# Mixer attention of a two-layer encoder: leaving out the TensorE products whose results are never read

## The reference, cut to what matters

```
u = rms_norm(x, g[MIX_PRE])
pa, pb, pc = jnp.split(u @ w_in[l], [split_b, split_c], axis=-1)
ya = neighbourhood_attn(qa * scale, ka, va, na_rpb[l])      # A: 6 heads
yb = hyena_mixer(pb, ...)                                   # B: 256 channels
yc = dilated_mixer(qc * scale, kc, vc, t5_table)            # C: 6 heads
y = jnp.concatenate([rms_norm(ya, ..), rms_norm(yb, ..), rms_norm(yc, ..)], axis=-1)
x = x + rms_norm(y @ w_out[l], g[MIX_POST])
```

## Time and profile before

| | |
|---|---|
| median of 3 runs | 2685.17 us (2684.04 to 2689.0) |
| the profiled execution: its own time | 2689.14 us |
| its span | 2687.3 us |
| mean granted TensorE clock of it | 0.98 of full speed |
| mixer attention, steps 2 to 54, layer 1 | about 632 to 739 us |
| mixer attention, steps 2 to 54, layer 2 | about 1960 to 2067 us |

### The profile page before, as it was taken

How to read it: one execution, slowest core, us unless ns; L and a number is a source line. 1 busy time by engine, 2 the same in 40 slices (tenths; PEclk the granted TensorE clock), 3 DMA queues, 4 the chain that set the end, 5 groups by cost and what they waited for, 6 DMA issues and landing times.

```text
span 2687.3 us, 47605 instructions
## 1 busy us (share of the span) xinstructions
PE 2585.8 (96%) x20484; PEld 2470.9 (92%) x20484; DVE 1027.3 (38%) x1351; ACT 923.3 (34%) x1509; POOL 112.9 (4%) x186
## 2 busy tenths in 40 slices
PE   7999997899999899999999999978999999999998
PEld 7999996698799799999999999966978998999998
DVE  3333236234445453332253332443443643533322
ACT  4333233024533343332253331331254433533322
POOL 0000000140000000000000000103200000000000
PEclk9999997999999999999999999979999999999999
DMA  4322324041024122333232322321300341233222
GB/s 147 94 93 94 99 75 156 22 138 48 1 94 139 52 96 94 94 95 98 87 111 94 94 94 95 117 95 48 136 25 25 102 142 40 95 94 94 94 95 79
DMA packets 66247, 240.62 MB, mean 90 GB/s; under 512 B 8882, under 2 KB 10632, under 8 KB 65088
## 3 DMA queue, kind: packets, MB, share of 16 engines
q1 hardware_dynamic: 57600, 209.74, 24.0%
q0 software_dynamic: 8368, 28.83, 3.3%
q10 hardware_dynamic: 144, 0.07, 0.0%
HBM read 236.48 MB, written 2.12 MB: 89 GB/s over the span
## 4 chain that ended last, share of the span: by engine, by line
PE 88%; DVE 6%; DMA 3%; ACT 2%; issue 1%; POOL 0%; DVEq 0%; ACTq 0%; POOLq 0%
PE bank L322 23%; PE bank L326 23%; PE bank L324 23%; PE bank L515 3%; DMA raw<-in_w_proj 2%; PE bank L490 2%; PE bank L376 2%; PE bank L378 2%; PE bank L377 2%; DVE wl L261 2%; PE bank L574 1%; PE bank L592 1%; PE bank L457 1%; PE bank L583 1%; PE bank L464 1%
## 5 line engine op out<-in xcount | busy, mean ns | idle before, releaser
L261 DVE TENSOR_TENSOR wl<-raw,wh 128x1024 fp32r<-128x1024 f32 x392 | 486.4, 1241 | 482.0 <-ACT wh L256 480.7
L322 PE MATMUL bank<-uH,wh 128*128 128x256 f32 x3328 | 664.4, 281 | 0.0
L326 PE MATMUL bank<-uH,wl 128*128 128x256 f32 x3328 | 661.1, 280 | 0.0
L324 PE MATMUL bank<-uL,wh 128*128 128x256 f32 x3328 | 660.9, 280 | 0.0
L256 ACT ACTIVATE wh<-raw 128x1024 fp32r<-128x1024 f32 x392 | 413.3, 1054 | 706.8 <-PE bank L326 586.1
L322 PEld LDWEIGHTS bank<-uH,wh 128*128 128x128 f32 x3328 | 507.5, 189 | 7.2 <-issue 7.1
L324 PEld LDWEIGHTS bank<-uL,wh 128*128 128x128 f32 x3328 | 507.2, 188 | 0.0
L326 PEld LDWEIGHTS bank<-uH,wl 128*128 128x128 f32 x3328 | 507.0, 188 | 0.0
L973 DVE TENSOR_TENSOR tmp<-bank,tmp 128x512 f32<-128x512 f32 x88 | 60.8, 691 | 629.5 <-PE bank L326 596.8
L322 PE MATMUL bank<-wh,hH 128*128 128x256 f32 x1408 | 281.6, 281 | 0.0
L326 PE MATMUL bank<-wh,hL 128*128 128x256 f32 x1408 | 281.1, 281 | 0.0
(11 more groups left out here) (198 smaller groups left out, 2959.0 us busy)
## 6 DMA issues: line engine op xcount, KB each, us to landing
raw<-in_w_first SPq DMA_DIRECT2D x176, 512.0 KB, 3.6
raw<-in_w_proj SPq DMA_DIRECT2D x128, 512.0 KB, 3.5
raw<-in_w_second SPq DMA_DIRECT2D x88, 512.0 KB, 3.5
strip<-bias_of_distance POOLq DMA_DIRECT2D x2, 2688.0 KB, 13.3
g_pre<-in_grow POOLq DMA_DIRECT2D x8, 512.0 KB, 7.2
g_post<-in_grow POOLq DMA_DIRECT2D x8, 512.0 KB, 4.9
fwd<-in_k_fwd POOLq DMA_DIRECT2D x4, 1024.0 KB, 7.0
inv<-in_k_inv POOLq DMA_DIRECT2D x2, 2048.0 KB, 9.4
```

Source lines behind the costliest of these rows:

```text
L261: e.tensor_tensor(wl[u % RING][:], raw[u % RAWS][:], wh[u % RING][:].bitcast(F32), ALU.subtract).then_inc(split_ready, 1)
L322: e.matmul(b[:, c], still_h, hi[:, c], start=first and c.start == 0, stop=False)
L324: e.matmul(b[:, c], still_h, lo[:, c], start=False, stop=False)
L326: mm = e.matmul(b[:, c], still_l, hi[:, c], start=False, stop=last and c.stop == n)
```

## The change

The two kinds of product whose results nobody reads are left out of the mixer attention: 3 x 5 products of 512 columns a layer (steps 2 to 6, with the wait ahead of them), and 40 products of `ones` with `eye` a layer. No other instruction, buffer or wait is touched.

```diff
@@ -32,7 +32,6 @@
 EMB = 33
 BIG = 1e30
-KEEP_BUSY = 3
 LOG_EXP_SET = 6
@@ -471,13 +470,6 @@
                         mm.then_inc(score_mm, 1)
-                    if part == "mixer" and 2 <= s < 7:
-
-
-                        w = wh[U_WO % RING]
-                        e.wait_ge(split_ready, L * UNITS + U_WO + 1)
-                        for _ in range(KEEP_BUSY):
-                            e.matmul(bank[7][:], w[:, 0:P], w[:, 0:T], start=True, stop=True)
                     s2 = s - 2
@@ -496,9 +488,6 @@
                         g = g0 + s3 // per
-                        if part == "mixer" and s3 % per:
-
-                            e.matmul(bank[4 + g % 2][:, 384:512], ones[:], eye[:], start=True, stop=True)
                         e.wait_ge(pt_ready, L * ITEMS + (t + 1))
```

## The result

The changed kernel takes 2803.51 us (median of 4 runs, 2802.88 to 2808.74), the kernel before 2684.61 us on the same chip: a ratio of 1.045, with a 95% interval of 1.0437 to 1.0463. It is slower by 119 us; 2799 had been forecast, within 2700 to 2835.

A forecast was written before the change was run, and what follows sets the result against it. PE, busy 96% of the span, bounds the kernel. A fallen clock adds 14.3, 39.9 and 2.9, that is 57 us a layer, 114 in both: 2799 us against the median, range 2700 to 2835.

The forecast's parts named there:

- The removed products are on PE's path: Mixer attention at unchanged clock: products of 512 columns in steps 4 to 6 and most ones products cost PE time.
- the prediction's first sum: Gain at an unchanged clock in the attention: 2.25 + 4.4 + 2.2 = 8.9 us a layer, 18 in all.
- The clock falls at about 637 to 640 in both layers: Start of the attention: with steps 2 and 3 bare, PE stands 1.7 us amid thin steps and the clock falls.
- each thin A step as a further occasion: A steps after the start: they stay thin for 20 steps, each offering the clock another chance to fall.
- The rows that the fall was argued from: Earlier profile: clock fell after 1.5 us standing at 1778.4 and after 1.10 of 3.10 us busy; 4.35 of 6.80 held.
- It doesn't come back before the output units: Attention after the fall: clock stays at 1.2 GHz, since gapless 64-row work, 7.15 of 7.20 us busy, stayed at 0.50.
- The price of a step: Attention steps at half clock: A steps of 1.39 us and C steps of 2.32 us, each times 1.8.
- The single factor of 1.8: Slowdown at 1.2 GHz for what PE issues, from a pair of products taking 0.43 against 0.24.
- The stretches of layer 1: Steps 4 to 23 plus 14.3 us, steps 24 to 47 plus 39.9, steps 48 to 50 plus 2.9.
- The sum: Both layers' attention: 57 us a layer longer, 114 in both.
- The clock holds: Rival: standing at 634 to 635.7 is too short to lower the clock; 18 us won, 2667 us, chance 0.12.
- Back in C: Rival: clock falls in A and returns in the fuller C steps; plus 10 us a layer, 2705 us, chance 0.07.

The follow-up runs named there:

- Experiment 1: Kernel before without the ones products, with the products of 512 columns kept: 2722.99 us, ratio 1.0133; one execution of four took 2771.24.
- experiment 4: Kernel before with products of 512 columns at steps 2 and 3 alone, all ones products kept: 2682.88 us, ratio 1.0001; one execution of ten at 2736.58.
- experiment 3: Kernel before with ones products for A items alone, none for C, products of 512 columns kept: 2678.39 us, ratio 0.9982; one execution of ten at 2731.89.
- experiment 2: Kernel before without the products of 512 columns, with the ones products kept: 2817.75 us, ratio 1.0478; one execution of four at 2798.79.
- experiment 5: Kernel before with all the extra products, same columns and counts, over 64 rows in place of 128: 2883.72 us, ratio 1.0726.
- experiment 7: Kernel before, plus two output tiles of each of the first two output units made around the last group's transposes, where PE stood: 2671.62 us, ratio 0.9962.
- experiment 6: Kernel before with the extra products replaced by transposes of the unit matrix over about the same time: 2683.61 us, ratio 1.0.

## Why the prediction was right, point by point

- *The removed products are on PE's path.* Right at a held clock. Experiment 1, layer 2, and experiment 4 show 5.8 and 2.2 us a layer; the prediction's first sum had 6.6 and 2.25. It is off a little in the ones of A (1.9 where 2.2 was counted) and more in those of C, whose last four bring little (experiment 3).
- *The clock falls at about 637 to 640 in both layers.* Right: 637.6 and 2026.9. PE stood for 1.73 us where 1.7 had been worked out. Experiments 1 and 2 show that this is the place: with the products of 512 columns alone it holds there, with the ones alone it doesn't. The four executions lie within 6 us, so the fall came in both layers each time; a layer that held would have shown as some 57 us less. The prediction also had each thin A step as a further occasion. That isn't borne out: in experiment 1 the A steps held in both layers, and one layer fell behind them.
- *The rows that the fall was argued from.* They carry less than the prediction put on them. The two stretches that it compares, 1.10 of 3.10 us busy and 4.35 of 6.80, are not of equal length. Over the like 3.1 us of layer 2 PE was busy for 1.09 us (the line below this list), so the same work with the same standing fell once and held once, already in the kernel before. And at 1778 the clock had only just come back: its mean from 1770 to 1778 is 0.80. So the fall of the changed kernel was judged from places on the edge, which these rows alone could not settle; that it came in all four executions is what the measurement added.
- *It doesn't come back before the output units.* Right in layer 1; in layer 2 it came back for 3.4 us in the last items. The reason given, that 64-row work at half clock doesn't bring it back, fits experiment 5, at 0.50 for 207 us of layer 1, and the 52 and 99.8 us of gapless work at 0.50 in the changed kernel. It isn't a law: experiment 2 came back in C.
- *The price of a step.* A: 2.50 forecast, 2.51 measured; C: 4.18 and 4.22. The single factor of 1.8 stood for 1.83 (A scores, 1.15 for 0.63), 1.78 (C scores, 1.58 for 0.89), 1.76 (C transposes) and 1.90 (values, 1.60 for 0.84). The values product, which had no row at half clock and was bounded between once and twice, lies near twice.
- *The stretches of layer 1.* Steps 4 to 23: plus 16.0 us (637.55 to 689.65), forecast 14.3; the 1.5 us allowed for steps still at full clock weren't there in layer 1, in layer 2 one such step is, at 1.44 us. Steps 24 to 47: plus 40.8 (689.65 to 790.15), forecast 39.9. From step 48 to the output: plus 2.8 (9.0 became 11.8), forecast 2.9 and no change.
- *The sum.* 114 us in both layers, 116.4 measured, and 3.2 us more outside the attention, which the prediction did not count and no run explains.
- *The rivals.* "The clock holds" is out: its place was right and its time, 2667, can't be had by leaving all out. With the products of 512 columns kept, experiment 1 shows it in one layer of two. The sentence of the Trainium skill that would have made it the outcome (TensorE: Matmul & The Clock Gate, section Why this matters for your kernels) judges by the length of idle gaps. The trace doesn't agree: gaps shorter than those it warns of, 1.73 us here and 0.75 in experiment 5, both amid thin work, were followed by a fall. "Back in C" is out for the changed kernel.

The stretch of layer 2 that is like the one at 926.9 to 930.0, in the kernel before:

```profile
2256.19:2259.29 3.10, 1.09 (x7) 0.88 (x8) 1.77 (x3) 0.79 (x2) 0.00 (x0) 1.00 0.00 0
```

What stays open: what decides whether a place on the edge, such as the passage from A to C in experiment 1, falls. The instructions were the same in both layers; the runs show no difference but their place in time. Nor is it shown which of the two things that the products of 512 columns do at the start, filling the wait or making the work around it denser, is the one that counts.

## What to carry to other kernels

A product whose result nobody reads may still hold the clock: before leaving one out, read the granted clock around it, and what PE would do in its place. Where PE stands or works thinly, real work moved into the gap (experiment 7) does the same for nothing, and a filler is needed only in the places where taking it out moves the clock. One execution doesn't tell that: in experiments 3 and 4 the profile showed a held clock and one of ten executions was over 50 us longer. Look at the single times, not at the median alone. A clock that falls ahead of a long thin stretch costs the whole stretch, 57 to 60 us a layer here for a gap of 1.7.

## What the runs showed of the hardware that I had not expected

- The clock can stay at 1.2 GHz for 167 us while PE is busy without a gap (experiment 2, layer 2), with this mix of 64-row scores, transposes and products of 64 and 128 columns.
- Transposes held the clock as well as products (experiment 6: 2683.61 us, ratio 1.0).
- The same extra columns over 64 rows, with 0.75 us of standing in place of 0.2, did not hold it (experiment 5). Such an fp32 product costs 1.02 us a step at half clock, against 0.43 over 128 rows: 0.72 itself, and 0.29 by which the values products behind it get longer. Why isn't shown.
- Identical layers of one execution can differ by 47 us (experiment 1: 150.8 and 103.7 us).
